# Second feed-forward on one core: down products whose weights move, sums seeded with the residual, and a result in token rows

## The reference

```python
x = x + mod_l[5] * swiglu(modulate(rmsnorm(x, ffn_norm_g[i]), mod_l[3], mod_l[4]),
                          ffn_w1[i], ffn_w3[i], ffn_w2[i])
...
return rmsnorm(x, final_g)
```

## Time and profile before

| what | value |
|---|---|
| time, median of three runs | 1701.12 us (1697.63 to 1703.18) |
| the profiled execution: its time | 1700.45 us |
| its span | 1698.7 us |
| granted TensorE clock, mean | 0.994 of full speed |
| PE busy / DVE / ACT / POOL | 98% / 69% / 54% / 44% of the span |
| second feed-forward, even part (1524 to 1685 us): DVE / ACT / POOL busy of 161 us | 90.7 / 85.6 / 89.9 us |

### The profile page before, as it was taken

The page is one execution under the profiler, slowest core; times in us unless marked ns, Lnnn a source line. Parts: engine busy times, 40 slices in busy tenths (PEclk is TensorE's granted clock), DMA queues, the critical chain, the costliest instruction groups (busy, mean ns, idle before and its releaser), DMA issues.

```text
span 1698.7 us, 31084 instructions
## 1 busy us (share of the span) xinstructions
PE 1663.0 (98%) x10720; PEld 1473.9 (87%) x10720; DVE 1172.8 (69%) x2104; ACT 923.0 (54%) x1511; POOL 755.3 (44%) x357
## 2 busy tenths in 40 slices
PE   9999999999999999999999999999999999999998
PEld 8878999988999998888888889958899988789997
DVE  3683379867777777777887776365755579675555
ACT  5463455577666665545545454264555563555554
POOL 4410668888999991000000004403455645235553
PEclk8999999999999999999999999999999999999999
DMA  6312565578555557888788863203555543146553
GB/s 223 108 42 91 172 209 179 182 268 287 169 177 183 176 171 238 294 288 290 286 287 294 291 229 110 88 13 121 166 187 184 185 150 124 55 158 187 185 185 123
DMA packets 86344, 312.39 MB, mean 184 GB/s; under 512 B 9843, under 2 KB 9843, under 8 KB 86131
## 3 DMA queue, kind: packets, MB, share of 16 engines
q1 hardware_dynamic: 85972, 309.38, 54.1%
q0 software_dynamic: 288, 1.97, 0.3%
HBM read 310.26 MB, written 1.05 MB: 183 GB/s over the span
## 4 chain that ended last, share of the span: by engine, by line
PE 84%; DVE 7%; ACT 3%; issue 3%; POOL 1%; DMA 1%; DVEq 0%; SPq 0%; POOLq 0%; ACTq 0%
PE psr L897 17%; PE psr L837 16%; PE psr L1152 10%; PE acc_all L1152 10%; PE psr L900 9%; PE acc_all L837 7%; PE psr L1099 3%; PE psr L1044 2%; DVE arena L2576 1%; DVE wl L570 1%; PE psr L784 1%; POOL wl L570 1%; ACT wh L561 1%; PE psr L935 1%; PE psr L825 1%
## 5 line engine op out<-in xcount | busy, mean ns | idle before, releaser
L570 POOL TENSOR_TENSOR wl<-ring,wh 128x1024 fp32r<-128x1024 f32 x276 | 673.2, 2441 | 563.3 <-ACT wh L561 557.3
L561 ACT ACTIVATE wh<-ring 128x1024 fp32r<-128x1024 f32 x470 | 494.8, 1054 | 298.6 <-PE psr L837 147.8
L897 PE MATMUL psr<-hb,wh 128*128 128x512 f32 x1344 | 343.5, 397 | 0.7 <-DVE hb L1998 0.7
L570 DVE TENSOR_TENSOR wl<-ring,wh 128x1024 fp32r<-128x1024 f32 x194 | 240.4, 1239 | 59.2 <-ACT wh L561 58.3
L897 PEld LDWEIGHTS psr<-hb,wh 128*128 128x128 f32 x1344 | 240.8, 189 | 45.6 <-DVE hb L1998 2.2
L837 PE MATMUL psr<-hb,wh 128*128 128x256 f32 x1584 | 212.5, 287 | 5.3 <-DVE hb L1995 3.1
L837 PEld LDWEIGHTS psr<-hb,wh 128*128 128x128 f32 x1584 | 200.0, 194 | 9.5 <-issue 3.8
L900 PEld LDWEIGHTS psr<-hb,wl 128*128 128x128 f32 x1344 | 182.7, 190 | 15.9 <-DVE wl L570 1.7
L1152 PE MATMUL acc_all<-wh,hb 128*128 128x512 f32 x504 | 196.1, 389 | 0.0
L1152 PE MATMUL psr<-wh,hb 128*128 128x512 f32 x504 | 196.1, 389 | 0.0
L900 PE MATMUL psr<-hb,wl 128*128 128x256 f32 x1344 | 187.7, 282 | 1.0 <-DVE wl L570 0.8
(11 more groups left out here) (381 smaller groups left out, 2744.6 us busy)
## 6 DMA issues: line engine op xcount, KB each, us to landing
ring<-in_peer_u SPq DMA_DIRECT2D x128, 512.0 KB, 3.5
ring<-in_peer_v SPq DMA_DIRECT2D x128, 512.0 KB, 5.0
sq<-in_ada_w SPq DMA_DIRECT2D x91, 512.0 KB, 4.2
ring<-in_ffn_a SPq DMA_DIRECT2D x44, 512.0 KB, 4.0
ring<-in_ffn_b SPq DMA_DIRECT2D x44, 512.0 KB, 3.5
ring<-in_ffn_d SPq DMA_DIRECT2D x44, 512.0 KB, 3.5
ring<-in_pw SPq DMA_DIRECT2D x24, 512.0 KB, 3.5
ring<-in_w_in SPq DMA_DIRECT2D x18, 512.0 KB, 3.5
```

Of the source, the lines that this page charges most:

```text
L561: nc.scalar.activation(wh[:, q % 2, :], ring[:, s, :], ACT.Copy).then_inc(high_ready, 1)
L570: eng.tensor_tensor(wl[:, q % 2, :], ring[:, n % NS, :], wh[:, q % 2, :], ALU.subtract)\
L897: mm(ps[:, :], wh[:, b, chunk(k)], hb[:, k, :, :], start=(k == 0), stop=False, skip_group_check=True)
```

## The change

The second feed-forward (layer 1) makes its down products with the operands exchanged: fgh and fgl, 128 tokens at a time, are the stationary operand and the weights move, 512 columns at a time (`token_product`, 12 matmuls in place of 24). acc then holds tokens x features. For this, three things move:

- The residual x is put into acc first: `seed_sums` transposes x by PE, 16 transposes of 128 x 128, between the sums and products of tile a(1, 0).
- The factor mod(1, 5) can no longer be applied per partition after the product. DVE multiplies every d tile in the ring by a row of it (`scale_down`, 128 x 1024, in place), before ACT makes the high part; ACT waits for `scaled`. The row is made by PE (8 matmuls in place of `keep_busy(9)`) and moved by ACT (`gate_row`).
- The last norm is per token: ACT squares and sums a token block straight from acc and makes its inverse root; DVE scales from acc to `result`. The squares' products `norm(12)`, the eight additions to x and `apply` are gone. The row of final_g, 512 KB, is loaded behind tile a(1, 2).

```diff
@@ -559,3 +559,6 @@
-            eng.wait_ge(tile_ready[s], at(it, per, lambda m: 16 * (m // NS + 1), n))
+            if TILES[n][0:2] == ("d", 1):
+                eng.wait_ge(scaled, at(it, per, lambda m: TILES[m][2] + 1, n))
+            else:
+                eng.wait_ge(tile_ready[s], at(it, per, lambda m: 16 * (m // NS + 1), n))
...
+                        if sums == 11:
+                            seed_sums(k)
+                            seed_sums(k + 1)
                         pe.wait_ge(raw_low, 4 * turn + k // 2 + 1)
...
+            def seed_sums(c):
+
+                pe.wait_ge(row_in, 1)
+                pe.wait_ge(x_added, X_ADDS["ffn0"] + c // 2 + 1)
+                for tb in range(TB):
+                    mm(acc[2 * tb + c // 4][:, c % 4 * P:(c % 4 + 1) * P], x[:, c, tb * P:(tb + 1) * P], ident,
+                       start=(c % 4 == 0), stop=False, is_transpose=True, skip_group_check=True)
...
+                    def products(acts, weights, stop=False):
+                        for tb in range(TB):
+                            for half in range(2):
+                                last = mm(acc[2 * tb + half][:, :], acts[:, f % 2, tb * P:(tb + 1) * P],
+                                          weights[:, b, half * 512:(half + 1) * 512], start=False, stop=stop,
+                                          skip_group_check=True)
+                        return last
+
+                    pe.wait_ge(high_ready, at(it, per, split_no, n) + 1)
+                    products(fgh, wh)
+                    products(fgl, wh)
+                    low_ready(pe, n, it, per)
+                    products(fgh, wl, stop=True).then_inc(tile_used, 1)
...
+                    for tb in range(TB):
+                        for acts, weights in ((fgh, wh), (fgl, wh), (fgh, wl)):
+                            for half in range(2):
...
+                        last.then_inc(block_done, 1)
...
-            keep_busy(9)
+            pe.wait_ge(rep_moved, 4 * len(PE_CONV))
+            for c in range(KC):
+                last = mm(acc[c // 4][:, c % 4 * P:(c % 4 + 1) * P], ada[:, 48 + 40 + c, 0:1].broadcast_to([P, P]), ident,
+                          start=True, stop=True)
+            last.then_inc(row_spread, 1)
...
+            act.wait_ge(row_spread, 1)
+            A(gate_row, acc_all[:, 0:D], ACT.Copy).then_inc(row_in, 1)
...
-            norm(12, x[:, :, :], KC, [], prev=("norm", 11), piece_ready=added(X_ADDS["pw2"], 2))
-            rootof(12)
+            for tb in range(TB):
+                act.wait_ge(block_done, tb + 1)
+                block_sum, block_root = small[:, 16 + tb:17 + tb], small[:, 18 + tb:19 + tb]
+                st.do(A(sq[:, tb * D:(tb + 1) * D], acc_all[:, tb * D:(tb + 1) * D], ACT.Square, accum_out=block_sum))
+                st.do(A(block_sum, block_sum, ACT.Ln, scale=1.0 / D, bias=eps))
+                A(block_root, block_sum, ACT.Exp, scale=-0.5).then_inc(token_root, 1)
...
+                def scale_down(f, it=None):
+                    if layer == 0:
+                        return
+                    n = TILE_NO["d", 1, f]
+                    s = n % NS
+                    dve.wait_ge(tile_ready[s], at(it, per, lambda m: 16 * (m // NS + 1), n))
+                    dve.wait_ge(row_in, 1)
+                    TT(ring[:, s, :], ring[:, s, :], gate_row, ALU.mult).then_inc(scaled, 1)
...
                             def second():
+                                scale_down(0)
                                 gated_low()
...
                             gated_low()
+                            scale_down(1)
...
+                    if it is not None or f < NF - 1:
+                        scale_down(f, it)
...
-            for q in range(4):
-                apply(x[:, 2 * q:2 * q + 2, :], h[:, 2 * q:2 * q + 2, :], par("final_g")[:, 2 * q:2 * q + 2], 2, final)
+            dve.wait_ge(row_loaded, 16)
+            for tb in range(TB):
+                dve.wait_ge(token_root, tb + 1)
+                for half in range(2):
+                    part = slice(half * 512, (half + 1) * 512)
+                    STT(out=result[:, tb, part], in0=acc[2 * tb + half][:, :], scalar=small[:, 18 + tb:19 + tb],
+                        in1=final_row[:, part], op0=ALU.mult, op1=ALU.mult).then_inc(final, 1)
```

More of the change, by code:

```diff
@@ L458, in build @@
         rep = a4["rep"].rearrange("p (h b n) -> p h b n", h=2, b=4)
+        gate_row, final_row = (a4["diag"][:, n * D:(n + 1) * D] for n in range(2))
+        result = a4["diag"][:, 2 * D:4 * D].rearrange("p (b n) -> p b n", b=TB)
         csig = a4["sig"].rearrange("p (b t) -> p b t", b=2)
@@ L747, in _ @@
                     n += 1
+                    if TILES[n - 1] == ("a", 1, 2):
+                        drained(sp, ("conv", PE_CONV[-1]))
+                        sp.dma_start(final_row, d["final_row"]).then_inc(row_loaded, 16)
             for q in range(4):
+                tb, part = q // 2, slice(q % 2 * 512, (q % 2 + 1) * 512)
                 sp.wait_ge(final, q + 1)
[L751 removed]
+                sp.dma_start(d["out"][tb * P:(tb + 1) * P, part], result[:, tb, part]).then_inc(out_stored, 16)
             sp.wait_ge(out_stored, 64)
@@ L1296, in down, with token_product, last_token_product @@
                                    for c in range(KC)], range(0, KC, 2) if f == 0 else (), it=it, per=per)
+                def token_product(f, it):
+                    n = TILE_NO["d", 1, f]
+                    b = split_no(n) % 2
+                    def products(acts, weights, stop=False):
[10 more added lines that the diff above has]
+                    products(fgh, wl, stop=True).then_inc(tile_used, 1)
+                def last_token_product():
+                    n = TILE_NO["d", 1, NF - 1]
+                    b, f = split_no(n) % 2, (NF - 1) % 2
+                    pe.wait_ge(fg_low, NF * (layer + 1))
+                    pe.wait_ge(high_ready, split_no(n) + 1)
+                    low_ready(pe, n)
+                    for tb in range(TB):
+                        for acts, weights in ((fgh, wh), (fgl, wh), (fgh, wl)):
+                            for half in range(2):
+                                last = mm(acc[2 * tb + half][:, :], acts[:, f, tb * P:(tb + 1) * P],
+                                          weights[:, b, half * 512:(half + 1) * 512], start=False, stop=(weights is wl),
+                                          skip_group_check=True)
+                        last.then_inc(block_done, 1)
                 def last_down():
@@ L1318, in ffn @@
                 over_ff(pe, step)
-                last_down()
+                if layer == 0:
+                    last_down()
+                else:
+                    last_token_product()
                 g_at[0] += 2 * NF
@@ L2475, in step @@
                         split_low(nc.vector, TILE_NO["d", layer, f - 1], it, per)
+                    if it is None and f == NF - 1:
+                        scale_down(f)
                     q = NF * layer + f + 1
@@ L2532, in ffn @@
                         .then_inc(x_added, 1)
-                    if layer == 0 and f % 2 and f >= 3:
+                    if f % 2 and f >= 3:
                         dve.wait_ge(x_added, f - 1)
```

32 lines of the change are left out of this document (19 added, 13 removed).

## The result

The changed kernel takes 1708.88 us (median of nine runs, 1704.85 to 1710.3), the kernel before, beside it, 1700.82 (nine runs, 1697.63 to 1703.18). The ratio is 1.0042, 95% interval 1.0032 to 1.0053: slower. Its profiled execution took 1706.57 us with a span of 1704.8, 6.1 more than the span before.

A forecast was written before the change was run, and what follows sets the result against it. PE was taken to bound the second feed-forward's even part. Seeds 1.8, entry 2.3, blocks 6.3, last block 1.85 and end -4.6 made +7.7 on 1700.45: 1708.1, or 1708.8 us at the median; range 1699.5 to 1716.

The forecast's parts named there:

- the down products: Second feed-forward: 12 matmuls of 512 columns take 2.72 us instead of 2.88, 0.16 less per block, 8.30 without new waits.
- The scaling in the even part: Blocks from down(2) to down(20): DVE's 1.23 us pass meets POOL's low part, 0.33 more per block, 6.3 in all.
- the mixed order: Even part: POOL gets the ports ahead of the scaling, always or in some blocks; forecast 1708.8 us, chance 0.35.
- DVE first throughout: Rival, even part: the scaling gets the ports ahead of POOL's b part in every block, 8.73 each; 1707.7 us, chance 0.20.
- E: Reference time in each block: the end of POOL's low part of the a tile, from which later steps are counted.
- POOL first: Even part: POOL's b part runs before the scaling, which ends at E + 3.7; d's high part is late, 8.84 per block.
- the covered case: Rival, even part: POOL's slack hides the scaling, needing a pass under 0.9 us; blocks 8.30, 1699.5 us, chance 0.17.
- Entry and seeds: Blocks 0 and 1: first scalings +1.05 and +1.41, less 0.16, so +2.3; 16 transposes on PE's path, +1.8.
- The collision: Rival at the entry: POOL's first b part gets the ports before DVE's low part of a(1, 2); 1715 us, chance 0.15.
- The row: The mod(1, 5) row: PE's products replace `keep_busy`, ACT's move is covered; 0 taken, at most 1.05 us uncovered.
- The last block: Behind down(20): the scaling stands between DVE's two low parts, so PE waits 2.3 us instead of 0.46, +1.85.
- The end: From the last product's start to the span's end: 8.9 us instead of 13.5, a gain of 4.6.

The follow-up runs named there:

- e1: Changed kernel without the 22 scalings of d tiles, ACT waiting only for the loaded tile; leaves out mod(1, 5): 1695.4 us, ratio 0.9962 to the kernel before.
- e3: Changed kernel with the scalings written to an unused buffer, ACT taking the unscaled tile without waiting; leaves out mod(1, 5): 1699.85 us.
- e8: Changed kernel with one more wait: POOL begins b's low part only once DVE has scaled the d tile, so DVE always goes first: 1715.36 us.
- e4: Changed kernel with each d tile scaled one block later on DVE, behind the addition of a's halves and ahead of d's low part: 1710.07 us.
- e2: Changed kernel scaling only the left 512 of 1024 columns of each d tile; the other half lacks the factor: 1695.92 us.
- e5: Changed kernel without the 16 transposes, each bank's first product starting its sum; leaves out the residual x: 1708.41 us.
- e7: As e6, but ACT's third-pair copies of x / mod(1, 5) stand behind b(1, 0)'s high part: 1694.39 us, ratio 0.9962 to the kernel before.
- e6: Changed kernel seeding sums with x / mod(1, 5), d tiles unscaled, acc multiplied by mod(1, 5) once at the end: 1698.75 us, ratio 0.998 to the kernel before.

## Why the prediction was right

**What bounds, and the down products: right.** PE alone set the pace, a down product got 0.16 shorter, and without the scaling each block is 8.31 (8.30 worked out). That the changed kernel gets none of it is shown by e1 against it.

**The scaling in the even part: right in mechanism, 0.02 per block too high.** "I take 0.33" per block; it was 0.31, 5.92 in all for 6.3. Both orders cost nearly the same, as worked out, and both occur: this is the forecast with the mixed order, and not DVE first throughout. The nearness to 0.33 is in part luck. From one E to the next it is 8.81 to 8.82 in the nine blocks with DVE first, for which 8.73 was worked out without the 0.1 that PE's products lose behind a wait; with POOL first it is 8.73 in six blocks and 8.81 in three, for 8.84. The two errors cancel in the mean. e3 shows that with POOL first the high part of d must wait for the scaling for there to be a price, e8 that with DVE first the low part of b carries it, and e4 that a third place without any meeting is no cheaper. e2 shows that the limit of the covered case lies between a pass of 0.68, which still costs 0.04 per block, and one of 1.21; the prediction put it at 0.9.

**Who goes first.** The scaling is ready when POOL's a part ends, and so is POOL's next. In the nine blocks that POOL won its part is recorded 50 to 71 ns ahead of the scaling, in the ten that DVE won 34 to 140 ns behind it; in e3 POOL is ahead by 48 to 246 ns, and wins, throughout. The Trainium skill's page "SBUF — State Buffer", section "SBUF: two separate sides", says that whoever starts first gets the ports for the whole instruction. By that rule and the recorded starts, the 19 blocks and those of e3 come out right; the prediction's argument against it rested on one pair 10 ns apart, too close to go by: in e2 DVE won twice with POOL recorded 4 ns ahead. The turn about is worked out from the two loops, not tested: a block with POOL first sends ACT's work to the next block in a different spacing from one with DVE first, and POOL then comes later or sooner by some 0.1.

**Entry and seeds: right.** Seeds 1.73 (e1) and 1.76 (e5) for 1.8. The scaling of d(0) cost 0.8 instead of 1.05 (15.77 from a(1, 0) to down(0) in e5 against 14.99), the stretch from down(0) to down(1) 1.61 more instead of 1.41 - 0.16: together 4.16 for 4.1. The collision did not come: POOL's first part is recorded 0.19 behind DVE's low part (1518.37 and 1518.18), as it was 0.20 behind it before. The row cost nothing, as taken: its move took 1.00 at 1474.90, and from PE's start of work at 1460.26 (1460.35 with the change) to a(1, 0) it is 35.29 before and 35.34 after. That the time ahead of this, too, agrees to 0.1 in the two traces is chance, since other executions differ there by several microseconds.

**The last block: mis-sized.** This is the term "+ 1.85": PE waited 0.68 longer than before, not 1.84. It was counted in the frame of POOL first, in which d(20) is scaled by E + 3.7 and everything up to the last product is in one queue of DVE behind it. Block 20 was one that DVE won: POOL's a part ended at E = 1687.28, the scaling was recorded at 1687.49 and took 1.22, and the low part of d(20) ended at 1690.56 + 1.49 = 1692.05, E + 4.8, where the prediction has E + 6.1. All behind it came 1.3 earlier. Where DVE has nothing early, in e4, from down(20) to the last product it is 4.99, close to the 5.06 of the prediction's frame. It is 4.46 in e2 and 4.57 in e3, where POOL was first in block 20, and 3.84 in e5 and 3.86 in the changed kernel and in e8, where DVE was. The step that was wrong is thus the order put in for block 20: the sum took POOL first for a single block, where the order alternates, and DVE was first.

**The end: right.** 8.85 for 8.9. Inside it two small errors cancel: the reading of the accumulator (0.19) and the two one-column passes (0.29 and 0.20, 0.52 from the start of one to the end of the other) stand between ACT's square and DVE, where 0.25 was allowed, and the stores were done sooner after DVE's last pass.

The sum, + 7.65 predicted and + 6.1 measured between the spans, is off by the last block (1.3 with the shorter product), the even part (0.4), and 0.14 the other way from the stages ahead. The medians of nine runs are 8.1 apart, so the 1708.8 forecast for the median and the 1708.88 measured agree better than the working deserves: the sum is 1.5 too high against the traces, and the medians lie 1.9 further apart than the two profiled executions. Where those 1.9 lie isn't shown; the earlier stages, which differ by more than that between executions, are the likely place.

## What to carry to other kernels

A pass on an engine that is idle for 40% of a stage is not free: look at where in the loop it would stand, who holds the ports at that moment, and which queue waits for its output; here 1.21 us of DVE cost 0.47 per block, and 0.68 in the same place cost 0.04. A factor that can't be taken out of a loop on one side of a sum can often be taken out on the other: dividing what the sum is seeded with and multiplying the sum once took no pass in the loop, for 2.1 more at the end (14.31 in e7 against 12.19 in e1). And place short work for the engine that feeds PE behind the part that PE waits for, not ahead of it.

## What the runs showed of the hardware

- A tie for the ports is decided within tens of nanoseconds and flips from block to block in a steady pattern: recorded start 50 to 71 ns ahead for POOL, or 34 to 140 ns behind, in otherwise equal blocks. Closer pairs don't follow the recorded start: in e2 DVE won at 0 and with POOL recorded 4 ns ahead, in the earlier trace rows POOL won when recorded 10 ns behind.
- In e6 PE stood for 1.90 us and then ran at the lower clock, and from a(1, 0) to down(1) it took 1.62 more than in e7, on top of the 0.81 of longer waiting. In e5 PE stood for 1.75 ahead of down(1), and the granted clock stayed at 1.00. Between e6 and e7 only the place of two copies differs; what in PE's idle time decides was not tried apart.
- Transposes of 128x128 fp32 cost 1.73 to 1.76 for 16 on PE's path, and 0.04 in all in e7, where PE's waits behind them shrank by as much.
